# Attention with the values stationary, two heads in the column halves of TensorE, and the division ahead of the transpose

## The chip, the cores and the metric

The kernel runs on one core of one Trainium2 chip. The metric is the device time of one execution in microseconds (us). Engines: PE (matmuls, and PEld for its weight loads), DVE (vector), ACT (scalar), POOL and SP (here they only issue DMAs). Each works through its own queue in order; they meet at semaphores.

## The reference, cut to what matters

Two layers work on 256 latent and 256 context tokens. Attention is one of three branches of the token mixer:

```
s = einsum('bqhd,bkhd->bhqk', q, k) * SOFTMAX_SCALE   # 8 heads, 96 deep
p = softmax(s, axis=-1)
o = einsum('bhqk,bkhd->bqhd', p, v)                   # v is 64 wide per head
```

Latent queries see all 512 keys, context queries only the 256 context keys. In layer 0 both kinds of queries are computed, in layer 1 only the latent ones. After the attention come the gMLP branch, gates, projections, and a dense SwiGLU (layer 0) or a top-2-of-8 mixture of experts (layer 1), all of them many f32-by-parts matmuls.

## The kernel before

Activations lie transposed: channels on partitions, tokens in the free direction. The projections run as weight-stationary tiles; each product is three fp32r matmuls (L650 to L652, high and low parts). Weights come by DMA into `raw`, ACT rounds them (`whi`, L1187), DVE makes the remainder (`wlo`, L1567). DVE also has the taps of a depthwise convolution (L1652) to do, a fixed number (`TAPS_UNIT`, 1 in layer 0 and 3 in layer 1) in each step of the attention.

The attention of a layer is a list of units (`UNITS`), one for a pair of heads j, a head h of the pair and a tile t of 128 queries, in the order j, h, t: 32 units in layer 0 (four tiles: two with 512 keys, two with 256), 16 in layer 1 (all 512 keys). A unit passes these stages:

- scores (PE, `scores`, L851): queries stationary, keys moving, into one of two banks `sc_bank`
- row maximum and its negative (DVE, L1771, L1772)
- exponential with the row sum (ACT, L1353) into `pr`, which has two buffers; it waits until the unit two before has been turned (`pt_psum`)
- reciprocal of the row sum (DVE, L1780) into `rinv`
- turn (PE, `turn`, L860): transposes of 128 columns each into the one bank `TB`; it waits for the exponential and for the copy of the last turned unit (`pt_ready`)
- copy of the turned block to `pT` (ACT, L1346), two buffers
- values (PE, `values`, L873): `pT` stationary, V (64 columns of one head) moving, out as queries x 64
- scaling by `rinv` on the way to `otok` (ACT, L1365)
- once for each pair of heads: the pair's outputs turned (PE, `outputs`, L882) into an accumulator bank, and split to `oh` (ACT, L1369) and `ol` (DVE, L1786) for the output projection

The stages are staggered by hand. In step s PE does scores(s), turn(s-2), outputs of a pair if it is complete, values(s-3), the query projection of the next pair (`queries`, in three steps of a layer), and in the first 24 steps of layer 0 and all 16 unit steps of layer 1 a piece of the modulation (`mod_chunk`, L750), whose rows are turned every eighth step (L759). ACT does in step s: the copy of turned unit s-2, the exponential of unit s, the scaling of unit s-3, the output's high part, then the query copies. DVE: maximum of s, reciprocal of s-1, taps, the output's low part, query rotation. Semaphore counts run on from layer 0 to layer 1 (`base_u`).

A form that matters later stands in the spatial step (L952): `vtok`, 64 columns wide, is stationary and its products go to the lower or the upper 64 partitions of a bank.

Of the kernel before, what the change touches and what calls it, by code (L numbers as in the profile page):

```python
# [135 lines left out]
def plan():  # L136
# [3 lines left out]
    for L in range(LAYERS):  # L140
# [8 lines left out]
        for j in range(4):  # L149
            chunks.append(("uq", L, j))  # L150
            accs += [("uq", L, j, h) for h in range(2)]
            if j == 0:
                chunks.append(("uv", L))
                accs += [("uv", L, t) for t in range(4)]

            if j > L:
                accs.append(("ot", L, j - 1 - L))
        accs += [("ot", L, j) for j in range(3 - L, 4)]
# [55 lines left out]
def build(nc, A, out):  # L214
    with ExitStack() as ctx:
# [81 lines left out]

        otok = place("otok", [P, 4, P], F32, std_at)
# [139 lines left out]
        ot_psum = sem("ot_psum")  # L438
# [65 lines left out]
        UNITS = {L: [(j, h, t) for j in range(4) for h in range(2) for t in range(live(L) // P)]  # L504
# [11 lines left out]

        def output_pair(L, s):

            j, r = divmod(s - 3, pair_units(L))
            return j - 1 if r == 0 and 1 <= j <= 4 else None  # L520
# [124 lines left out]
        def _(pe):  # L645
# [119 lines left out]
            for L in range(LAYERS):  # L765
# [75 lines left out]
                def scores(u):  # L841
                    j, h, t = units[u]
                    if (h, t) == (0, 0):
# [10 lines left out]
                def turn(u):  # L854
                    lo, hi = keys_of(units[u][2])
                    pe.wait_ge(exp_ready, base_u + u + 1)
# [6 lines left out]
                def values(u):  # L863
                    j, h, t = units[u]
                    lo, hi = keys_of(t)
                    nk = (hi - lo) // P
                    if u == 0:
                        taken(pe, ("uv", L, 3))
                    pe.wait_ge(pt_ready, base_u + u + 1)
                    if base_u + u >= 2:  # L870
                        pe.wait_ge(o_ready, base_u + u - 1)
                    for i in range(nk):
                        mm = pe.matmul(o_bank[u % 2][:, 0:VH], pT[:, u % 2, i * P:(i + 1) * P],  # L873
                                       V[:, lo // P + i, (2 * j + h) * VH:(2 * j + h + 1) * VH],
                                       start=(i == 0), stop=(i == nk - 1))
                    mm.then_inc(o_psum, 1)

                def outputs(j):
                    pe.wait_ge(o_ready, base_u + (j + 1) * pair_units(L))
                    b = bank(("ot", L, j))  # L880
                    for t in range(nq // P):
                        mm = pe.transpose(b[:, t * P:(t + 1) * P], otok[:, t, :], ident[:])  # L882
                    mm.then_inc(ot_psum, 1)
# [14 lines left out]
                for s in range(len(units) + 4):  # L898
                    if s < len(units):
                        scores(s)  # L900
                    if 2 <= s <= len(units) + 1:
                        turn(s - 2)
                    if output_pair(L, s) is not None:
                        outputs(output_pair(L, s))
                    if 3 <= s <= len(units) + 2:
                        values(s - 3)
# [268 lines left out]
        def _(act):  # L1175
# [74 lines left out]
            for L in range(LAYERS):  # L1250
# [86 lines left out]
                for s in range(len(units) + 4):  # L1337
                    if s and s % KD == 0 and s // KD <= len(MOD_ATT[L]):
                        copy_rows(MOD_ATT[L][s // KD - 1])
                    if 2 <= s <= len(units) + 1:  # L1340
                        u = s - 2
                        lo, hi = keys_of(units[u][2])
                        act.wait_ge(pt_psum, base_u + u + 1)
                        if base_u + u >= 2:
                            act.wait_ge(o_psum, base_u + u - 1)
                        nc.scalar.copy(pT[:, u % 2, 0:hi - lo], TB[:, 0:hi - lo]).then_inc(pt_ready, 1)  # L1346
# [9 lines left out]
                    out_j = output_pair(L, s)  # L1356
                    if out_j is not None:

                        act.wait_ge(ot_psum, 4 * L + out_j + 1)
                    if 3 <= s <= len(units) + 2:  # L1360
                        u = s - 3
                        j, h, t = units[u]
# [804 lines left out]
```

## Time and profile before

| | |
|---|---|
| median of 3 runs | 2468.6 us (2468.12 to 2473.57) |
| the profiled execution | 2469.17 us, span 2467.2 us |
| PE busy | 2354.1 us (95%) |
| DVE busy | 1715.1 us (70%) |
| ACT busy | 1358.4 us (55%) |
| attention of layer 0 | from 145.36 us to 236.76 us of the span |
| attention of layer 1 | from 1054.17 us to 1118.25 us of the span |

Busy time is the union of an engine's instructions. A matmul's end is modelled and matmuls overlap in the pipeline, so what a group of matmuls costs is read from the start of one group to the start of the next, not from its duration. Clock 1.00 is 2.4 GHz, 0.50 is 1.2 GHz.

### The profile page before, as it was taken

How to read it: one execution, taken by the hardware profiler on the slowest of the kernel's cores; microseconds unless marked ns; L12 is line 12 of the kernel's file. 1: busy time of each engine (PE TensorE's matmuls, PEld its weight loads, DVE VectorE, ACT ScalarE, POOL GpSimd, SP SyncE). 2: the span in 40 equal slices, each digit the busy share in tenths (PEclk: the TensorE clock that was granted, in tenths of full speed). 3: DMA queues.
4: the chain of work that ended last, by engine and by line, in shares of the span. 5: the costliest groups of instructions: out<-in, count | busy, mean ns of one | idle time of the engine just before them, and what ended most of it. 6: DMA issues, size and time to landing. Idle time of an engine off the chain costs nothing.

```text
span 2467.2 us, 32689 instructions
## 1 busy us (share of the span) xinstructions
PE 2354.1 (95%) x12370; PEld 1921.1 (78%) x12370; DVE 1715.1 (70%) x1796; ACT 1358.4 (55%) x1438; POOL 46.1 (2%) x87
## 2 busy tenths in 40 slices
PE   6989999998999998898997999999999999999997
PEld 3757778876788885767995888888888888888886
DVE  4867753426333336777657989898989898989895
ACT  3366343234222234546446777777777777777773
POOL 0010000001000000010000000000000000000000
PEclk9999999999999999999997999999999999999999
DMA  7243123345422233433655999999999999999992
GB/s 281 86 138 125 59 98 102 116 163 207 141 96 94 95 102 121 153 129 124 197 215 199 368 350 365 346 361 358 364 346 367 346 369 352 361 351 362 346 369 105
DMA packets 103249, 569.02 MB, mean 231 GB/s; under 512 B 11760, under 2 KB 13680, under 8 KB 54640
## 3 DMA queue, kind: packets, MB, share of 16 engines
q1 hardware_dynamic: 91632, 525.72, 57.4%
q0 software_dynamic: 11520, 41.95, 4.7%
q8 instruction: 67, 1.10, 0.2%
q14 instruction: 30, 0.25, 0.0%
HBM read 566.58 MB, written 1.05 MB: 230 GB/s over the span
## 4 chain that ended last, share of the span: by engine, by line
PE 88%; DVE 6%; ACT 3%; issue 1%; SPq 1%; DMA 1%; DVEq 0%; ACTq 0%
PE bank L650 26%; PE bank L651 26%; PE bank L652 26%; PE bank L851 1%; PE bank L1070 1%; PE bank L873 1%; PE bank L1136 1%; PE bank L750 1%; DVE hres L1627 1%; PE bank L860 1%; DMA mod_s<-in_mod 1%; DVE y L1624 1%; DVE cacc L1652 1%; DVE wlo L1567 1%; SPq L545 0%
## 5 line engine op out<-in xcount | busy, mean ns | idle before, releaser
L1894 DVE TENSOR_TENSOR elo<-eraw,ehi 128x2048 fp32r<-128x2048 f32 x378 | 862.4, 2288 | 131.7 <-ACT ehi L1239 130.7
L1239 ACT CAST ehi<-eraw 128x2048 fp32r<-128x2048 f32 x378 | 722.6, 1915 | 246.1 <-PE bank L652 241.8
L1567 DVE TENSOR_TENSOR wlo<-raw,whi 128x1024 fp32r<-128x1024 f32 x220 | 269.5, 1225 | 244.4 <-ACT whi L1187 242.6
L650 PE MATMUL bank<-ah,whi 128*128 128x512 f32 (+1 forms) x1088 | 395.4, 363 | 12.2 <-DVE wlo L1567 6.5
L650 PE MATMUL bank<-ehi,xgh 128*128 128x512 f32 x1008 | 399.4, 396 | 1.7 <-DVE xgl L1900 1.2
L651 PE MATMUL bank<-elo,xgh 128*128 128x512 f32 x1008 | 393.4, 390 | 0.0
L652 PE MATMUL bank<-ehi,xgl 128*128 128x512 f32 x1008 | 393.0, 390 | 0.0
L651 PE MATMUL bank<-al,whi 128*128 128x512 f32 (+1 forms) x1088 | 389.9, 358 | 0.0
L652 PE MATMUL bank<-ah,wlo 128*128 128x512 f32 (+1 forms) x1088 | 389.8, 358 | 0.0
L1187 ACT CAST whi<-raw 128x1024 fp32r<-128x1024 f32 x220 | 229.3, 1043 | 117.5 <-PE bank L652 117.1
L650 PEld LDWEIGHTS bank<-ah,whi 128*128 128x128 f32 x1088 | 207.7, 191 | 47.4 <-DVE wlo L1567 10.2
L651 PEld LDWEIGHTS bank<-al,whi 128*128 128x128 f32 x1088 | 207.9, 191 | 30.5 <-issue 1.4
L652 PEld LDWEIGHTS bank<-ah,wlo 128*128 128x128 f32 x1088 | 207.8, 191 | 29.9
L652 PEld LDWEIGHTS bank<-ehi,xgl 128*128 128x128 f32 x1008 | 189.5, 188 | 41.0
L650 PEld LDWEIGHTS bank<-ehi,xgh 128*128 128x128 f32 x1008 | 189.6, 188 | 40.5 <-DVE xgl L1900 1.4
L651 PEld LDWEIGHTS bank<-elo,xgh 128*128 128x128 f32 x1008 | 189.6, 188 | 37.5
L650 PE MATMUL bank<-ehi,hTh 128*128 128x512 f32 x504 | 197.1, 391 | 1.5 <-DVE hTl L2019 1.5
L652 PE MATMUL bank<-ehi,hTl 128*128 128x512 f32 x504 | 196.2, 389 | 0.0
L651 PE MATMUL bank<-elo,hTh 128*128 128x512 f32 x504 | 196.0, 389 | 0.0
L1652 DVE SCALAR_TENSOR_TENSOR cacc<-up,par,cacc 128x512 f32<-128x512 f32 (+1 forms) x240 | 140.7, 612 | 3.1
L650 PEld LDWEIGHTS bank<-ehi,hTh 128*128 128x128 f32 x504 | 94.6, 188 | 21.0 <-issue 1.7
L652 PEld LDWEIGHTS bank<-ehi,hTl 128*128 128x128 f32 x504 | 94.6, 188 | 19.8
(268 smaller groups left out, 2685.1 us busy)
## 6 DMA issues: line engine op xcount, KB each, us to landing
eraw<-in_moe SPq DMA_DIRECT2D x378, 1024.0 KB, 5.1
raw<-in_dense SPq DMA_DIRECT2D x220, 512.0 KB, 3.3
mod_a<-in_mod POOLq DMA_DIRECT2D x40, 512.0 KB, 4.2
mod_b<-in_mod POOLq DMA_DIRECT2D x40, 512.0 KB, 7.5
mod_s<-in_mod SPq DMA_DIRECT2D x16, 512.0 KB, 13.5
hres<-in_xT SPq DMA_DIRECT2D x1, 2048.0 KB, 8.0
wsT<-in_wsT SPq DMA_DIRECT2D x2, 512.0 KB, 3.5
out_h<-hres SPq DMA_DIRECT2D x2, 512.0 KB, 2.9
```

What stands on the lines that cost most here:

```text
L650: pe.matmul(dst, wh, xh, start=first, stop=False, skip_group_check=True)
L651: pe.matmul(dst, wh, xl, start=False, stop=False, skip_group_check=True)
L652: return pe.matmul(dst, wl, xh, start=False, stop=last, skip_group_check=True)
L750: mm = pe.matmul(b[32 * j:32 * j + 32, :], cst[:, k, :], w[:, 256 * j:256 * j + 256], start=(k == 0), stop=(k == KD - 1), skip_group_check ...
L851: pe.matmul(sc_bank[u % 2][:, 0:hi - lo], qT_of(j)[:, h, t * P:(t + 1) * P], kT[:, 2 * j + h, lo:hi], start=True, stop=True).then_inc(sc_r ...
L860: mm = pe.transpose(TB[:, i * P:(i + 1) * P], pr[:, u % 2, i * P:(i + 1) * P], ident[:])
L873: mm = pe.matmul(o_bank[u % 2][:, 0:VH], pT[:, u % 2, i * P:(i + 1) * P], V[:, lo // P + i, (2 * j + h) * VH:(2 * j + h + 1) * VH], start= ...
L1187: nc.scalar.copy(whi[c % SPLIT][:], raw[c % RAW][:]).then_inc(w_hi, 1)
L1239: nc.scalar.copy(ehi[c % ESPLIT][:], eraw[c % ERAW][:]).then_inc(e_hi, 1)
L1567: dve.tensor_tensor(wlo[c % SPLIT][:], raw[c % RAW][:], whi[c % SPLIT][:].bitcast(F32), ALU.subtract).then_inc(w_lo, 1)
L1652: ins = dve.scalar_tensor_tensor(acc, src, w, acc, ALU.mult, ALU.add)
L1894: dve.tensor_tensor(elo[c % ESPLIT][:], eraw[c % ERAW][:], ehi[c % ESPLIT][:].bitcast(F32), ALU.subtract).then_inc(e_lo, 1)
```

## The change

- Units come in the order j, t, h: both heads of a pair for one tile of queries follow each other. In layer 0 four units with 512 keys are followed by four with 256.
- The exponentials are scaled by `rinv` in place (ACT, with its own semaphore `pn_ready`) before they are turned. The turn waits for that instead of the exponential.
- Values handles two units at once, in even steps from step 4: V is stationary (64 columns), `pT` moves (128 columns), head 0 goes to the lower 64 partitions of the output bank and head 1 to the upper ones. The output is then already channels x queries.
- `outputs`, `otok` and the accumulator banks for it are gone. ACT copies the bank to `oh` for each pair of units, DVE subtracts to `ol`.
- ACT's order in a step: exp(s), scale(s-1), copy of turned s-2, output copy (even steps). DVE's: reciprocal(s-1), maximum(s), output remainder (odd steps from 5), taps. PE's: scores(s), values (even steps), turn(s-2), queries, modulation.
- The loop has one step less.

```diff
-UNITS = {L: [(j, h, t) for j in range(4) for h in range(2) for t in range(live(L) // P)]
+UNITS = {L: [(j, h, t) for j in range(4) for t in range(live(L) // P) for h in range(2)]
          for L in range(LAYERS)}
...
         def turn(u):
             lo, hi = keys_of(units[u][2])
-            pe.wait_ge(exp_ready, base_u + u + 1)
+            pe.wait_ge(pn_ready, base_u + u + 1)
             if base_u + u:
                 pe.wait_ge(pt_ready, base_u + u)
             for i in range((hi - lo) // P):
                 mm = pe.transpose(TB[:, i * P:(i + 1) * P], pr[:, u % 2, i * P:(i + 1) * P], ident[:])
             mm.then_inc(pt_psum, 1)
 
-        def values(u):
-            j, h, t = units[u]
+        def values(m):
+
+            j, _, t = units[2 * m]
             lo, hi = keys_of(t)
             nk = (hi - lo) // P
-            if u == 0:
+            if m == 0:
                 taken(pe, ("uv", L, 3))
-            pe.wait_ge(pt_ready, base_u + u + 1)
-            if base_u + u >= 2:
-                pe.wait_ge(o_ready, base_u + u - 1)
+            pe.wait_ge(pt_ready, base_u + 2 * m + 2)
+            if base_u // 2 + m >= 2:
+                pe.wait_ge(o_ready, base_u // 2 + m - 1)
             for i in range(nk):
-                mm = pe.matmul(o_bank[u % 2][:, 0:VH], pT[:, u % 2, i * P:(i + 1) * P],
-                               V[:, lo // P + i, (2 * j + h) * VH:(2 * j + h + 1) * VH],
-                               start=(i == 0), stop=(i == nk - 1))
+                for h in range(2):
+                    mm = pe.matmul(o_bank[m % 2][64 * h:64 * h + 64, 0:P],
+                                   V[:, lo // P + i, (2 * j + h) * VH:(2 * j + h + 1) * VH],
+                                   pT[:, h, i * P:(i + 1) * P], start=(i == 0), stop=(i == nk - 1),
+                                   skip_group_check=True)
             mm.then_inc(o_psum, 1)
-
-        def outputs(j):
-            pe.wait_ge(o_ready, base_u + (j + 1) * pair_units(L))
-            b = bank(("ot", L, j))
-            for t in range(nq // P):
-                mm = pe.transpose(b[:, t * P:(t + 1) * P], otok[:, t, :], ident[:])
-            mm.then_inc(ot_psum, 1)
 
         base_u = 0 if L == 0 else len(UNITS[0])
...
-        for s in range(len(units) + 4):
+        for s in range(len(units) + 3):
             if s < len(units):
                 scores(s)
+            if s >= 4 and s % 2 == 0:
+                values(s // 2 - 2)
             if 2 <= s <= len(units) + 1:
                 turn(s - 2)
-            if output_pair(L, s) is not None:
-                outputs(output_pair(L, s))
-            if 3 <= s <= len(units) + 2:
-                values(s - 3)
             if s and query_pair(L, s) is not None:
                 queries(query_pair(L, s))
...
-        for s in range(len(units) + 4):
+        for s in range(len(units) + 3):
             if s and s % KD == 0 and s // KD <= len(MOD_ATT[L]):
                 copy_rows(MOD_ATT[L][s // KD - 1])
-            if 2 <= s <= len(units) + 1:
-                u = s - 2
-                lo, hi = keys_of(units[u][2])
-                act.wait_ge(pt_psum, base_u + u + 1)
-                if base_u + u >= 2:
-                    act.wait_ge(o_psum, base_u + u - 1)
-                nc.scalar.copy(pT[:, u % 2, 0:hi - lo], TB[:, 0:hi - lo]).then_inc(pt_ready, 1)
             if s < len(units):
 
                 lo, hi = keys_of(units[s][2])
...
                 nc.scalar.activation(pr[:, s % 2, 0:hi - lo], sc_bank[s % 2][:, 0:hi - lo], ACT.Exp,
                                      bias=negmax[:, s % 2:s % 2 + 1], scale=SCALE,
                                      accum_out=rsum[:, s % 2:s % 2 + 1]).then_inc(exp_ready, 1)
-            out_j = output_pair(L, s)
-            if out_j is not None:
-
-                act.wait_ge(ot_psum, 4 * L + out_j + 1)
-            if 3 <= s <= len(units) + 2:
-                u = s - 3
-                j, h, t = units[u]
+            if 1 <= s <= len(units):
+                u = s - 1
+                lo, hi = keys_of(units[u][2])
                 act.wait_ge(rinv_ready, base_u + u + 1)
-                act.wait_ge(o_psum, base_u + u + 1)
-                nc.scalar.activation(otok[:, t, 64 * h:64 * h + 64], o_bank[u % 2][:, 0:VH], ACT.Copy,
-                                     scale=rinv[:, u % 4:u % 4 + 1]).then_inc(o_ready, 1)
-            if out_j is not None:
-                b = acc_bank[ACC[("ot", L, out_j)] % 2]
-                nc.scalar.copy(oh[:, out_j, 0:nq], b[:, 0:nq]).then_inc(x_hi, 1)
+                nc.scalar.activation(pr[:, u % 2, 0:hi - lo], pr[:, u % 2, 0:hi - lo], ACT.Copy,
+                                     scale=rinv[:, u % 4:u % 4 + 1]).then_inc(pn_ready, 1)
+            if 2 <= s <= len(units) + 1:
+                u = s - 2
+                lo, hi = keys_of(units[u][2])
+                act.wait_ge(pt_psum, base_u + u + 1)
+                if base_u + u >= 2:
+                    act.wait_ge(o_psum, (base_u + u) // 2)
+                nc.scalar.copy(pT[:, u % 2, 0:hi - lo], TB[:, 0:hi - lo]).then_inc(pt_ready, 1)
+            if s >= 4 and s % 2 == 0:
+                m = s // 2 - 2
+                j, _, t = units[2 * m]
+                act.wait_ge(o_psum, base_u // 2 + m + 1)
+                nc.scalar.copy(oh[:, j, t * P:(t + 1) * P], o_bank[m % 2][:, 0:P]).then_inc(x_hi, 1)
             if s and query_pair(L, s) is not None:
                 take_queries(query_pair(L, s))
...
         taps(TAPS_IN["uv"][L])
         for s in range(len(units) + 4):
+            if 1 <= s <= len(units):
+                u = s - 1
+                dve.wait_ge(exp_ready, base_u + u + 1)
+                if base_u + u >= 4:
+
+                    dve.wait_ge(pn_ready, base_u + u - 3)
+                dve.reciprocal(rinv[:, u % 4:u % 4 + 1], rsum[:, u % 2:u % 2 + 1]).then_inc(rinv_ready, 1)
             if s < len(units):
                 lo, hi = keys_of(units[s][2])
                 i = s % 2
...
                 chain(dve.tensor_reduce(rowmax[:, i:i + 1], sc_bank[i][:, 0:hi - lo], AX.X, ALU.max))
                 dve.tensor_scalar(negmax[:, i:i + 1], rowmax[:, i:i + 1], -SCALE, None,
                                   ALU.mult).then_inc(negmax_ready, 1)
-            if 1 <= s <= len(units):
-                u = s - 1
-                dve.wait_ge(exp_ready, base_u + u + 1)
-                if base_u + u >= 4:
-
-                    dve.wait_ge(o_ready, base_u + u - 3)
-                dve.reciprocal(rinv[:, u % 4:u % 4 + 1], rsum[:, u % 2:u % 2 + 1]).then_inc(rinv_ready, 1)
+            if s >= 5 and s % 2 == 1:
+                m = (s - 5) // 2
+                j, _, t = units[2 * m]
+                dve.wait_ge(x_hi, n.next(x_hi))
+                dve.tensor_tensor(ol[:, j, t * P:(t + 1) * P], o_bank[m % 2][:, 0:P],
+                                  oh[:, j, t * P:(t + 1) * P].bitcast(F32), ALU.subtract).then_inc(o_ready, 1)
             taps(TAPS_UNIT[L])
-            out_j = output_pair(L, s)
-            if out_j is not None:
-                dve.wait_ge(x_hi, n.next(x_hi))
-                a = ACC[("ot", L, out_j)]
-                dve.tensor_tensor(ol[:, out_j, 0:nq], acc_bank[a % 2][:, 0:nq],
-                                  oh[:, out_j, 0:nq].bitcast(F32), ALU.subtract).then_inc(acc_free[a % 2], 1)
             if s and query_pair(L, s) is not None:
                 turn_queries(query_pair(L, s))
         modulation(L, *((16, 40), (32, 48))[L])
```

## Rows read from the trace of the kernel before

**Rows 1.** The chain of waits of the whole run, share of the span by engine.

```profile
PE 88%; DVE 6%; ACT 3%; issue 1%; SPq 1%; DMA 1%; DVEq 0%; ACTq 0%
```

**Rows 2.** Windows of both stages: length, busy PE, PEld, DVE, ACT, POOL; granted clock; DMA.

```profile
145.36:236.76 91.40, 88.43 (x629) 61.55 (x627) 64.70 (x160) 55.25 (x152) 11.13 (x21) 0.98 0.42 141
...
1054.17:1118.25 64.08, 58.90 (x424) 40.32 (x422) 54.99 (x137) 32.49 (x81) 6.89 (x13) 0.95 0.43 147
```

**Rows 3.** Timeline of PE, layer 0: start, duration (us), engine, line, operation, count.

```profile
178.23 0.60 PE L860 MATMUL bank<-ident,pr 128*128 128x128 f32 x4
178.66 0.60 PE L882 MATMUL bank<-ident,otok 128*128 128x128 f32 x4
...
181.79 1.00 PE L873 MATMUL bank<-V,pT 128*128 128x64 f32 x8
182.72 0.64 PE L750 MATMUL bank<-mod_a,cst 128*32 128x256 f32 x8
183.29 1.12 PE L851 MATMUL bank<-kT,qT 96*128 96x512 f32 x2
184.25 0.38 PE L860 MATMUL bank<-ident,pr 128*128 128x128 f32 x2
```

**Rows 4.** Timeline, spatial step of layer 0, PE alone.

```profile
302.87 1.09 PE L952 MATMUL bank<-wsT,vtok 128*64 128x128 f32 x16 [1.00 <-DVE uT L1825]
...
303.89 0.50 PE L650 MATMUL bank<-ah,whi 128*128 128x512 f32 x1
```

**Rows 5.** Groups of ACT by form, 145 to 312: busy us, mean ns, idle before.

```profile
L1353 ACT ACTIVATE pr<-bank,negmax 128x512 f32<-128x512 f32 x16 | 11.0, 688 | 8.2 <-DVE negmax L1772 8.2
...
L1346 ACT COPY pT<-bank 128x512 f32<-128x512 f32 x16 | 9.4, 586 | 6.5 <-PE bank L860 6.2
L1353 ACT ACTIVATE pr<-bank,negmax 128x256 f32<-128x256 f32 x16 | 7.7, 481 | 4.4 <-PE bank L860 2.9 <-DVE negmax L1772 1.4
...
L1346 ACT COPY pT<-bank 128x256 f32<-128x256 f32 x16 | 6.0, 372 | 11.5 <-PE bank L860 11.5
...
L1388 ACT ACTIVATE vT<-vT,par 128x512 f32<-128x512 f32 x4 | 2.9, 808 | 0.0
...
L1402 ACT CAST gmh<-uT 128x512 fp32r<-128x512 f32 x4 | 2.5, 621 | 8.0 <-DVE uT L1825 8.0
```

**Rows 6.** Timeline of ACT, layer 0: two instructions that follow each other.

```profile
223.21 0.31 ACT L1365 ACTIVATE otok<-bank,rinv 128x64 f32<-128x64 f32 x1
223.41 0.58 ACT L1346 COPY pT<-bank 128x512 f32<-128x512 f32 x1
```

**Rows 7.** Timeline, later in layer 0: transposes after a wait, and their reader.

```profile
292.05 0.66 PE L943 MATMUL bank<-ident,vT 128*128 128x128 f32 x4 [0.68 <-ACT vtok L1394]
292.75 0.59 ACT L1394 COPY vtok<-bank 128x512 f32<-128x512 f32 x1 [0.74 <-PE bank L943]
```

**Rows 8.** Timeline, layer 0: maximum and exponential of the scores at 183.29.

```profile
184.45 0.69 DVE L1771 TENSOR_REDUCE rowmax<-bank 128x1 f32<-128x512 f32 x1 [1.07 <-PE bank L851]
...
185.37 0.69 ACT L1353 ACTIVATE pr<-bank,negmax 128x512 f32<-128x512 f32 x1 [0.32 <-DVE negmax L1772]
```

**Rows 9.** Timeline of ACT: exp(0) of layer 0, exp(2) of layer 1.

```profile
150.22 0.69 ACT L1353 ACTIVATE pr<-bank,negmax 128x512 f32<-128x512 f32 x1 [2.48 <-DVE negmax L1772]
...
1067.74 0.69 ACT L1353 ACTIVATE pr<-bank,negmax 128x512 f32<-128x512 f32 x1 [3.44 <-DVE negmax L1772]
```

**Rows 10.** Timeline: first query matmul and next exponential, layer 0, then layer 1.

```profile
160.97 0.48 PE L650 MATMUL bank<-cnh,whi 128*128 128x512 f32 x1
...
169.04 0.47 ACT L1353 ACTIVATE pr<-bank,negmax 128x256 f32<-128x256 f32 x1 [1.45 <-DVE negmax L1772]
...
1076.97 0.36 PE L650 MATMUL bank<-cnh,whi 128*128 128x256 f32 x1
...
1083.71 0.69 ACT L1353 ACTIVATE pr<-bank,negmax 128x512 f32<-128x512 f32 x1 [1.66 <-DVE negmax L1772]
```

**Rows 11.** Windows, a stretch early in layer 1's attention; columns as in Rows 2.

```profile
1068.00:1077.00 9.00, 8.34 (x37) 5.73 (x37) 6.57 (x20) 4.30 (x12) 0.53 (x1) 0.62 0.35 119
```

More of the change, by code:

```diff
@@ L154, in plan @@
                 accs += [("uv", L, t) for t in range(4)]
-            if j > L:
-                accs.append(("ot", L, j - 1 - L))
-        accs += [("ot", L, j) for j in range(3 - L, 4)]
         for s in ("gv", "gu"):
@@ L296, in build @@
         qT2 = place("qT2", [QK_HEAD, 2, TOK], F32, wsT_at)
-        otok = place("otok", [P, 4, P], F32, std_at)
         uT = place("uT", [P, 4, TOK], F32, w1)
@@ L437, in build @@
         o_ready = sem("o_ready")
-        ot_psum = sem("ot_psum")
+        pn_ready = sem("pn_ready")
         vt_ready = sem("vt_ready")
@@ L515, in query_pair @@
             return j if r == 0 and 1 <= j < 4 else None
-        def output_pair(L, s):
-            j, r = divmod(s - 3, pair_units(L))
-            return j - 1 if r == 0 and 1 <= j <= 4 else None
         def qT_of(j):
@@ L842, in scores @@
                     j, h, t = units[u]
-                    if (h, t) == (0, 0):
+                    if (t, h) == (0, 0):
                         taken(pe, ("uk", L, 3))
```

## The prediction

> **What bounds the kernel now.** I read the chain of waits first: 88% of it is PE [rows 1]. The busy times of the two stretches that the change touches, the attention of layer 0 and of layer 1, come next: PE is busy for 88.4 of 91.4 us and 58.9 of 64.1 us, ACT for 55.2 and 32.5 [rows 2]. So PE sets the pace of attention in layer 0, and nearly so in layer 1. In the timeline of PE one step is scores, turn, values and a piece of modulation, back to back: eight value matmuls (512 keys) hold PE 0.93 us, a modulation piece 0.57 [rows 3]. I call what PE does for 512 keys L and for 256 keys S; layer 0 has 16 of each, layer 1 has 16 L.
>
> **The part that gets cheaper.** Values of two heads become 16 matmuls on 64-column halves. The form exists already in the spatial step: 16 such instructions start at 302.87 and the next full-width matmul starts at 303.89, so 1.02 us for a pair L where 2 x 0.93 were spent [rows 3, 4]. For a pair S I take 0.59, eight instructions less at (1.09 - 0.27)/15 = 0.054 us (0.27 is an estimate of the last one's own tail). PE work saved: layer 0 8 x 0.84 + 8 x 0.35 = 9.5 us, layer 1 8 x 0.84 = 6.7. The turns of the outputs go: four transposes are 0.43 us when nothing is waited for [rows 3], about 1.8 us in layer 0; in layer 1, where PE stops for the last scaling ahead of them, I estimate 3 us with that stop. Together 21 us of PE's time. The question is whether PE still is what is waited for.
>
> The row of the 64-column form has its change of layout in it: the next weight load starts only when the 16 have left the array, while between full-width matmuls a load is drawn ahead. The Trainium skill (TensorEngine Tiling (Array Packing), Key Properties) says that changing the tiling mode drains the array; the trace agrees. Without such a drain a pair L would cost 16 x 0.054 = 0.86 and the sum below would be 24 x 0.16 = 3.8 us less.
>
> **The part that gets slower: one chain through ACT.** In the new order ACT does in step s: exp(s), scale(s-1), the copy of the turned block pT(s-2), and in even steps the copy of an output. Three waits close this to a ring. exp(s) overwrites the buffer of unit s-2, so it waits for turn(s-2). turn(s-2) waits for the copy pT(s-3), since there is one bank for turned blocks, and for scale(s-2). Both stand behind exp(s-1) in ACT's queue. Before, the copy stood ahead of the exponential, so that ring was only turn and copy. Now no two steps overlap: turn(u-1) -> exp(u+1) -> scale(u) -> pT(u-1) -> turn(u). In even steps the values of a pair stand on PE between the copy and the turn, and need that copy, so they are in the ring too. What stands behind ACT's wait: everything of the next step, and through exp, DVE's reciprocal, behind which the next row maximum now stands.
>
> The terms, L / S. Exponential 0.69 / 0.48, copy of the turned block 0.59 / 0.37 [rows 5]. Scale, SBUF to SBUF in place with one scale column: the trace has no such row. The plain cast from SBUF is 0.62, the activation from SBUF with both a scale and a bias column is 0.81, so one column is half of the way, 0.72 [rows 5]; an ACT instruction that nobody waits for lets the next one start 0.11 us before its end (otok 0.31 long, next one 0.20 later) [rows 6], so 0.61 of ACT's queue; for S I estimate 0.39. Bounds: 0.20 (the 64-column scale, same operation) and 0.81. A turn that starts after a wait, to the start of ACT's work on it: 292.05 to 292.75, 0.70 [rows 7]; S two transposes less, 0.48. From ACT to PE 0.05.
>
> - L after L, odd unit: 0.70 + 0.69 + 0.61 + 0.59 + 0.05 = 2.64; even unit, with values: 3.66. A pair L takes 6.30 us.
> - S after S: 0.48 + 0.48 + 0.39 + 0.37 + 0.05 = 1.77, with values 2.36.
> - The mixed ones of a group of eight (four L, four S): 2.43, 3.23, 1.98, 2.79. One group: 20.9 us.
>
> PE's own work for a pair L is 2 x 0.96 scores, 2 x 0.43 turns, 1.02 values, 2 x 0.57 modulation = 4.9 us, so it is idle for a fifth even where it has modulation to do. The way over the row maximum, 1.16 us from the start of the scores to the reduction and 0.92 from there to the exponential [rows 3, 8], is at 0.59 + 0.57 + 2.08 = 3.2 us after the turn's start, against 0.70 + 2.64 = 3.3 on the ring: hidden, but only just. Where an L follows an S it is late by 0.5, with a modulation's row turn ahead of it by 1.0; I add 3 us in layer 0 and 0.4 in layer 1. DVE's reciprocal ahead of the reduction costs nothing: exponential to exponential through DVE is 0.8 + 0.05 + 0.08 + 0.92 = 1.85.
>
> **Layer 0.** exp(0) stays at 150.22 [rows 9]; the reciprocal and maximum behind it put exp(1) at 152.0, its scale(0) ends at 153.4, and the first turn starts at 153.5, 8.1 us into the stage. Four groups 83.4, less the last interval (2.8) and the exponential missing at the end (0.7): 79.9. Queries three times: they start 0.43 after a turn, and from their first matmul to the next exponential it is 8.07 (160.97 to 169.04), since ACT and DVE must turn the queries first [rows 10]; to the next turn 1.29 more. Together 9.8 us in place of 3.23 + 1.77, so 4.8 each, 14.4. Row maximum 3. End: copy, values S, 1.5 us, and no turn of outputs. Sum 8.1 + 79.9 + 14.4 + 3.0 + 1.5 = 106.9 against 91.4 [rows 2]: +15.5 us.
>
> **Layer 1.** exp(2) is at 1067.74 [rows 9], 0.6 later with scale(0) ahead of the query copies; turn(1) follows at 1070.25, 16.1 us into the stage. PE waits for it, and its granted clock is low afterwards, as it already is there today (0.62 over 1068 to 1077 [rows 11]); a turn and values at half rate on the ring add 1.9. Seven pairs 44.1 less 0.7. Two queries inside: 0.43 + 6.74 (1076.97 to 1083.71) [rows 10] + 1.94 = 9.1 in place of 6.3, 5.6 together. Row maximum 0.4, end 2.4. Sum 16.1 + 1.9 + 43.4 + 5.6 + 0.4 + 2.4 = 69.8 against 64.1: +5.7.
>
> **Moved but free.** DVE's subtractions become 24 of 128 columns where there were 8 larger ones; they stand in steps where DVE waits for the scores. ACT's output copy runs beside the next turn. The accumulator banks lose four users in a layer, which keeps their alternation for all later work. SP and POOL lose nothing: POOL's modulation fetches follow PE's pieces with 3 buffers. After attention PE is the bound again, and its weights, ACT's rounding and DVE's remainders all hang on it, so a later end moves everything by its full amount.
>
> Total +21.2 us on the profiled execution (2469.2 us, span 2467.2): 2490. The median of the runs shown, 2468.6, is 0.6 lower, so I say 2490.
>
> **Rivals.**
> 1. PE stays the bound, the ring hides. Then the 21 us of PE work come off: 2469 - 21 = 2448. For it: PE is 97% busy in layer 0 now, ACT 60%. Against: ACT's order leaves it nothing to do while it waits for the turn. It would need a step L of at most 2.4 us on average where the ring has 3.15. Chance 0.06.
> 2. The scale costs no more than the 64-column one. 48 x 0.41 = 20 us come off: 2470, no change. For it: the same operation; against: all of ACT's rows grow with their columns, 0.37 to 0.59 for the copy. Chance 0.06.
> 3. PE's clock falls as well. The ring leaves PE 20 to 40% idle. The granted clock is 0.98 and 0.95 of 2.4 GHz over the stages today [rows 2], and 0.62 where PE had waited for exp(2) of layer 1, which itself waited 3.4 us for its maximum [rows 9, 11]. At 1.2 GHz throughout, turns and values on the ring would add 20 us in layer 0 and 14 in layer 1: 2524; in parts of the stages, 2500. Chance of more than 10 us of it: 0.16.
> 4. The forecast, 2480 to 2498: 0.72. Its own range is made by the scale's cost (48 x 0.15 = 7 us either way), the drain (4) and shorter drops of the clock.
>
> **The numbers.** Likeliest 2490. The range reaches down by the cheaper scale and halves to 2476 and up into the third rival to 2503. A measurement of this kernel can tell 0.2% (5 us) from no change. Faster than that: rival 1, 0.06, and a bit of 2, 0.01. The same: 0.05 from rival 2. Slower: 0.88.
>
> **What would show it.** In the timeline after, exp(s) starts right after turn(s-2) in every step, and the copy pT is the last thing before each turn; waits of ACT for the turn, over 20 us in layer 0; PE waiting for pT and for the scaled block, which it hardly does today. A pair L 6.3 us from turn to turn, values 1.0 us for a pair, the scale 0.7 us. Stages of 107 and 70 us. It is wrong if PE is still over 90% busy in the stages, if a scale is under 0.4 us, or if the later stages take back part of the delay.

## The result and the profile after

The changed kernel takes 2507.2 us (median of four, 2500.4 to 2518.5) against 2470.5 for the kernel before (median of four, 2468.1 to 2473.6): ratio 1.0152, 95% interval 1.0136 to 1.0168. It is slower, as forecast, but by 37 us where 21 had been forecast, and lies beyond the range's upper end of 2503. The profiled execution took 2507.76 us, with a span of 2505.9.

| | before | after | forecast |
|---|---|---|---|
| stage of layer 0 | 91.4 | 120.0 | 106.9 |
| stage of layer 1 | 64.1 | 77.1 | 69.8 |
| the rest of the span | 2311.7 | 2308.8 | as before |

A stage runs from the first scores to the first matmul of the next part. The delay is all in these two stages. First their windows, with a stretch of each kind (columns as in [rows 2]), then the chain of waits (as [rows 1]):

```profile
144.44:264.42 119.98, 97.47 (x611) 51.29 (x609) 68.37 (x171) 63.51 (x164) 11.08 (x21) 0.85 0.33 109
1082.10:1159.20 77.10, 62.08 (x416) 33.66 (x414) 55.61 (x139) 38.29 (x85) 6.86 (x13) 0.85 0.37 127
172.00:184.00 12.00, 11.16 (x48) 4.71 (x48) 5.28 (x15) 5.40 (x18) 1.58 (x3) 0.57 0.43 132
204.00:216.00 12.00, 11.82 (x56) 4.82 (x55) 5.17 (x13) 4.74 (x14) 1.58 (x3) 0.58 0.38 120
157.00:172.00 15.00, 12.36 (x100) 7.71 (x92) 8.80 (x23) 8.47 (x21) 2.11 (x4) 1.00 0.36 123
```

```profile
PE 86%; DVE 6%; ACT 5%; issue 2%; SPq 1%; DMA 1%; DVEq 0%; ACTq 0%
```

PE was busy for 97% of layer 0's stage and is now for 81%. The granted clock, 0.98 and 0.95 in [rows 2], is 0.85 in both stages. It isn't low everywhere: over 157 to 172 it is 1.00, over 172 to 184 and 204 to 216, both behind a block of queries, 0.57 and 0.58, so most of those stretches ran at 1.2 GHz. That is the first sign of what the forecast left out.

The ring is there as forecast. The groups of ACT by form, layer 0, which answer to [rows 5]:

```profile
L1336 ACT ACTIVATE pr<-pr,rinv 128x512 f32<-128x512 f32 x16 | 11.3, 709 | 0.0
L1329 ACT ACTIVATE pr<-bank,negmax 128x512 f32<-128x512 f32 x16 | 11.0, 687 | 26.8 <-PE bank L849 15.0 <-DVE negmax L1759 11.8
L1344 ACT COPY pT<-bank 128x512 f32<-128x512 f32 x16 | 9.1, 572 | 0.0
L1336 ACT ACTIVATE pr<-pr,rinv 128x256 f32<-128x256 f32 x16 | 8.0, 497 | 0.0
L1329 ACT ACTIVATE pr<-bank,negmax 128x256 f32<-128x256 f32 x16 | 7.6, 473 | 24.9 <-PE bank L849 16.2 <-DVE negmax L1759 8.7
```

The scale is 709 ns where I had taken 0.72 us. ACT, idle 8.2 and 4.4 us before its exponentials in [rows 5], is now idle 26.8 and 24.9. Most of it, 31 us, waits for the turn, as the ring has it, but 20.5 wait for the row maximum. Two steps of the ring at full clock, PE and ACT in layer 0:

```profile
184.26 0.66 PE L864 MATMUL bank<-pT,V 128*64 128x128 f32 x8
184.85 0.66 PE L849 MATMUL bank<-ident,pr 128*128 128x128 f32 x4
...
185.60 0.69 ACT L1329 ACTIVATE pr<-bank,negmax 128x512 f32<-128x512 f32 x1 [1.39 <-PE bank L849]
...
186.28 0.71 ACT L1336 ACTIVATE pr<-pr,rinv 128x512 f32<-128x512 f32 x1
...
186.89 0.57 ACT L1344 COPY pT<-bank 128x512 f32<-128x512 f32 x1
...
187.61 0.63 PE L849 MATMUL bank<-ident,pr 128*128 128x128 f32 x4 [0.48 <-ACT pT L1344]
...
188.33 0.69 ACT L1329 ACTIVATE pr<-bank,negmax 128x512 f32<-128x512 f32 x1 [0.70 <-PE bank L849]
...
190.25 1.09 PE L864 MATMUL bank<-pT,V 128*64 128x128 f32 x16 [0.81 <-ACT pT L1344]
191.27 0.44 PE L849 MATMUL bank<-ident,pr 128*128 128x128 f32 x2
```

Turn, exponential, scale, copy, turn: 187.61 - 184.85 = 2.76 us where 2.64 was forecast. With the values, 191.27 - 187.61 = 3.66, as forecast. The same kind of steps after a block of queries:

```profile
175.21 1.06 PE L840 MATMUL bank<-kT,qT 96*128 96x512 f32 x1
176.20 1.12 PE L864 MATMUL bank<-pT,V 128*64 128x128 f32 x8
177.25 0.69 PE L849 MATMUL bank<-ident,pr 128*128 128x128 f32 x2
177.73 0.86 PE L748 MATMUL bank<-sel,modrow 128*128 128x8 f32 x4
178.52 1.08 PE L739 MATMUL bank<-mod_a,cst 128*32 128x256 f32 x8
179.54 2.08 PE L840 MATMUL bank<-kT,qT 96*128 96x512 f32 x2
181.41 0.64 PE L849 MATMUL bank<-ident,pr 128*128 128x128 f32 x2
```

Every PE row is about twice as long: scores 2.0 us, a piece of the modulation 1.0. This S step takes 181.41 - 177.25 = 4.16 us where the forecast has 1.98, and 1.0 for the modulation's row turn in it. PE has no gap in it: turn 0.48, row turn 0.79, piece 1.02, scores 1.87. With the clock held up (the shorter extra matmuls below) the same two turns are at 174.23 and 176.69, 2.46 apart, with one extra matmul of 0.22 between them.

### The profile page after: what moved, and what is told of

It is laid out like the page before. It is cut to its first block, busy times and chain, and to the rows that moved or that the text cites. A ratio compares the mean times of both kernels' runs of the same rounds, so it can differ in the third digit from the quotient of the medians.

```text
span 2505.9 us, 32587 instructions
## 1 busy us (share of the span) xinstructions
PE 2364.8 (94%) x12346; PEld 1901.5 (76%) x12346; DVE 1719.8 (69%) x1812; ACT 1371.3 (55%) x1454; POOL 45.9 (2%) x87
## 4 chain that ended last, share of the span: by engine, by line
PE 86%; DVE 6%; ACT 5%; issue 2%; SPq 1%; DMA 1%; DVEq 0%; ACTq 0%
PE bank L639 26%; PE bank L641 25%; PE bank L640 25%; PE bank L1053 1%; PE bank L1119 1%; PE bank L849 1%; PE bank L864 1%; PE bank L840 1%; DVE hres L1607 1%; ACT pr L1336 1%; PE bank L739 1%; DVE wlo L1547 1%; ACT pT L1344 1%; DMA mod_s<-in_mod 1%; DVE y L1604 1%
## 5 line engine op out<-in xcount | busy, mean ns | idle before, releaser
L639 PEld LDWEIGHTS bank<-ah,whi 128*128 128x128 f32 x1088 | 207.9, 191 | 49.0 <-DVE wlo L1547 10.2
L639 PE MATMUL bank<-ehi,hTh 128*128 128x512 f32 x504 | 197.1, 391 | 1.5 <-DVE hTl L1999 1.5
```

The costliest lines, as they stand in the source:

```text
L639: pe.matmul(dst, wh, xh, start=first, stop=False, skip_group_check=True)
```

## The experiments

Each version below the first row was timed in five rounds beside the kernel before, whose median lay at 2470.4 to 2471.2. Stages, in us, are from the windows of each version's one profiled execution.

| | kernel, us | ratio (95%) | stage 0 | stage 1 |
|---|---|---|---|---|
| as changed | 2507.2 | 1.0152 (1.0136 to 1.0168) | 120.0 | 77.1 |
| extra matmuls on PE, long | 2498.3 | 1.0114 (1.0100 to 1.0129) | 114.5 | 70.6 |
| extra matmuls, shorter | 2495.2 | 1.0087 (1.0070 to 1.0105) | 109.3 | 69.7 |
| third buffer | 2502.5 | 1.0133 (1.0118 to 1.0148) | 114.3 | 75.8 |
| scores one step earlier | 2509.9 | 1.0152 (1.0137 to 1.0167) | 118.8 | 79.1 |
| both | 2476.8 | 1.0023 (1.0014 to 1.0032) | 94.3 | 67.1 |
| third buffer, chunk first | 2488.1 | 1.0065 (1.0051 to 1.0079) | 108.4 | 77.5 |
| scale of one column | 2490.9 | 1.0085 (1.0072 to 1.0098) | 110.0 | 70.2 |
| copy, scale, exp | 2464.2 | 0.9977 (0.9969 to 0.9986) | 88.8 | 61.2 |
| the same, scores earlier | 2539.6 | 1.0270 (1.0245 to 1.0294) | 135.2 | 87.3 |
| the same, extra matmuls | 2459.5 | 0.9950 (0.9936 to 0.9963) | 88.4 | 58.2 |
| division on DVE | 2472.6 | 1.0009 (1.0000 to 1.0018) | 88.8 | 68.0 |
| before, extra matmuls | 2463.2 | 0.9964 (0.9950 to 0.9977) | 89.6 | 60.8 |

### Is it the clock?

```
+ def warm(s, k):
+     for _ in range(k):
+         pe.matmul(b[:, 384:512], ident[:], ident[:], ...)
  scores(s)
+ warm(s, spare(s))        # s >= 2; and 12 (4) ahead of scores(2)
  values(s // 2 - 2); turn(s - 2)
```

> The changed kernel with extra fp32 matmuls of 128 columns (0.147 us each at the full clock, written to a part of a bank nobody reads) put on PE where it stands idle in the attention stages: 12 before scores(2), 5 after it, 8 before the turn that follows a query block, 4 or 2 in the steps with modulation, 7 in those without, in layer 1 up to 18; 80% of the measured idle time at most. Theory A (the ring through ACT costs what was forecast, and the 17 us beyond the forecast are steps run at PE's 1.2 GHz level, into which PE falls because it idles): the windows of the attention stages show a granted clock near 1.00, layer 0's stage takes about 107 us instead of 120.0, layer 1's 72 instead of 77, and the kernel 2490 us. Rival B (the low clock is no cause: the ring has a cost not counted, such as the row maximum behind the scores): the stage stays at 118 us or more and the kernel at 2507 or above, slower by what the extra matmuls get in the way.

Measured: the clock is 1.00 in both stages, and the kernel is at 2498.3, between the two theories. Layer 1's stage is 70.6 (Theory A: 72), layer 0's 114.5 instead of 107. In the window of layer 0 PE was busy for 112.7 of 114.5 us, which left no room: an extra matmul takes 0.245 us, and 0.147, the price of a transpose, had been used. (In this version they also start a new sum in the bank that holds the modulation's running sums, and this version computes another result; the versions below only add to theirs. The Trainium skill, PSUM — Partial Sum Buffer, The four PSUM rules, says that a starting matmul clears the marks of the whole bank, whichever bytes it writes; no run here shows that by itself, since the next version also has fewer of them.) So it was repeated with fewer:

```
- spare(s): 8 behind a query block, 4 or 2 with a chunk, 7 without; 12 ahead of scores(2)
+ spare(s): 5, 2 or 1, 3; 8 ahead of scores(2)
- start=True, stop=True
+ start=False, stop=False
```

> The changed kernel with extra matmuls on PE again, now by their measured length (0.245 us for each, where 0.147 had been counted, so that the earlier version had PE busy for 128 of 130 us and stood in its own way): 2 ahead of the values, 1 ahead of the other turns, 5 in the step behind a query block, 3 in the steps without modulation, 8 ahead of scores(2) in layer 0. Theory A (half of the excess over the forecast is PE at its lower level): layer 0's stage 107 to 110 us (120.0 as changed, 114.5 with the longer filling), layer 1's 70 to 71, the kernel 2488 to 2493. Rival B (the longer filling took all that the clock had to give): 2498 again or more.

```profile
144.31:253.62 109.31, 98.61 (x761) 65.51 (x759) 67.83 (x171) 63.53 (x164) 11.08 (x21) 1.00 0.36 120
1069.57:1139.28 69.71, 61.96 (x505) 39.90 (x503) 55.73 (x139) 38.30 (x85) 6.86 (x13) 1.00 0.41 139
```

These are the two stages: 109.3 and 69.7 us at clock 1.00, as Theory A has them. More work on PE makes the stages 18.1 us shorter, 197.1 to 179.0. That leaves 2.4 us of layer 0's excess over the forecast and, since the forecast of 69.8 has 1.9 us of half clock in it, 1.8 us in layer 1. The whole kernel came out at 2495.2, 12.0 us below the changed kernel and 2 us above what Theory A gave. The 18.1 us are those of the profiled execution, one of the two shortest; the five runs spread from 2488.0 (the profiled one, mean clock 0.986) to 2496.2 (0.983), and where the longer ones lost 7 us no trace shows.

### Which link closes the ring?

```
- exp(s) into pr[s % 2], waits for turn(s-2)
+ exp(s) into one of three buffers, waits for turn(s-3)
```

> The changed kernel with a third buffer for the exponential (in the space that the outputs' tile had before the change), so that exp(s) waits for turn(s-3) and not for turn(s-2); ACT's order stays. Theory A (the ring is closed by exp's wait for the buffer, and ACT's order inside it): the link is cut, exp(s) starts right after the last copy, ACT's own work of 0.69 + 0.71 + 0.57 + 0.14 = 2.1 us a step is below PE's 2.7, and the kernel is at 2450 to 2465 as with the other order. Rival B (ACT's added work): 2498 or above. Rival C (the buffer is not what exp waits for, but the copy's place behind exp and scale): between the two, 2480 to 2495.

Theory A fell here. Rival B's number came, 2502.5, but not for its reason, ACT's added work. The group rows of ACT (its exponential, in two of the buffers) say why:

```profile
L1333 ACT ACTIVATE pr<-bank,negmax 128x512 f32<-128x512 f32 (+1 forms) x22 | 12.8, 583 | 30.1 <-DVE negmax L1763 30.1
...
L1333 ACT ACTIVATE prc<-bank,negmax 128x512 f32<-128x512 f32 (+1 forms) x10 | 5.8, 582 | 13.6 <-DVE negmax L1763 13.6
```

No wait for the turn is left, and all 43.7 us are for the row maximum, which waits for the scores, which stand on PE behind the last turn. There are two rings of nearly one length. The forecast had worked out both, 3.2 and 3.3 us from a turn to the next step's exponential, and called the second "hidden, but only just"; I should have seen that cutting the longer one buys only the difference. The other link alone, and then both:

```
- for s: scores(s);   values(..); turn(s-2); chunk
+ scores(0); for s: scores(s+1); values(..); turn(s-2); chunk
```

> The changed kernel with PE's scores one step earlier: scores(s+1) ahead of values and turn(s-2), where scores(s+1) stood behind turn(s-2) and the modulation's chunk. Theory A2 (two rings of the same length: one through exp's wait for its buffer, 6.3 us for two L steps; one through PE's order, copy, values 1.02, turn 0.59, chunk 0.57, scores 1.06, row maximum 0.9, exp 0.67, scale 0.62, copy 0.57, together 6.1 to 6.2): this cuts the second alone, the first still holds, 2495 to 2505, exp waits for the turn at nearly every step and no longer for the row maximum. Rival B (only the ring through the row maximum is real, the other is its shadow): PE bound again, 2455 to 2470.

> The changed kernel with both: scores one step earlier and the third buffer for the exponential. Theory A2: both rings are cut, and ACT's order of the change (exp, scale, copy) costs nothing by itself; PE is the bound where there is modulation, the stage of layer 0 is 88 to 93 us and the kernel 2458 to 2470, as with ACT's other order (2464). Rival B (there is a third link, such as the reciprocal ahead of the row maximum on DVE, or ACT's own work): 2480 or more, and the idle rows before exp name it.

```profile
L1330 ACT ACTIVATE pr<-bank,negmax 128x512 f32<-128x512 f32 (+1 forms) x32 | 18.6, 581 | 49.9 <-PE bank L849 37.7 <-DVE negmax L1760 12.2
```

```profile
144.60:238.91 94.31, 83.17 (x611) 46.46 (x610) 66.40 (x171) 64.05 (x164) 11.10 (x21) 0.96 0.44 141
1060.18:1127.23 67.05, 55.67 (x416) 31.39 (x414) 54.91 (x139) 39.02 (x85) 6.87 (x13) 0.90 0.42 146
```

The first row is the exponential with the scores earlier alone: 37.7 us of waiting for the turn, the first ring. The kernel is at 2509.9, a little worse than forecast, since scores(3) now stands on PE ahead of the first turn, which moves from 7.9 to 10.3 us into layer 0's stage. The windows are those of both edits: 2476.8, with stages of 94.3 us, where 88 to 93 had been expected, and 67.1. One cut alone gives back 5 us or none, both give 30. The kernel does 0.2% worse than before, above Theory A2's number and under Rival B's; the later first turn, here too 10.3 us into the stage, is part of it.

The third buffer once more, with the second ring shortened instead of cut:

```
- for s: scores(s); values(..); turn(s-2); queries; chunk
+ for s: scores(s); chunk; values(..); turn(s-2); queries
```

> The changed kernel with the third buffer (2502 by itself) and the modulation's chunk ahead of values and turn in PE's order, where it stood behind them. Theory A2 (with the third buffer the ring that holds is copy, values, turn, chunk, scores, row maximum, exp, scale, copy, 6.2 us for two L steps): the chunk, 0.57 a step, leaves that ring and fills PE's wait, 24 steps in layer 0 and 16 in layer 1; one chunk is in the ring per two steps, so 0.57 for each of 20 pairs, 11 us, and some 5 more because PE idles less and keeps its clock: 2483 to 2492. Rival B (the chunk had been hidden): 2500 again.

2488.1, as Theory A2 has it: with the third buffer, what PE does between copy and scores is part of the length of the second ring. The profiled execution is the slowest of six (2502.8, the others 2486.5 to 2490.3), so its windows in the table don't stand for the median.

### What the scale costs

```
- activation(pr[:, u % 2, 0:n], pr[:, u % 2, 0:n], Copy, scale=rinv)
+ activation(pr[:, u % 2, 0:1], pr[:, u % 2, 0:1], Copy, scale=rinv)
```

> The changed kernel with the scaling cut to one column of 512 or 256 (leaves the division of the other columns out; every wait and signal stays). Theory A: the ring loses 0.6 us in an L unit and 0.4 in an S unit, some 26 us over both layers, L odd 2.0 and even 3.05, pair L 5.1 under PE's 5.5: PE bound again where there is modulation, the clock stays up, and the kernel is at 2455 to 2475. Rival B (the turn's wait for the exponential's buffer and the copies alone hold the stage): 2490 or above.

This version leaves the division of all other columns out. 2490.9: 16 us come back, less than the 26 of Theory A, and Rival B's number, if only just. The clock is 0.86 and 0.85 in the two stages, unmoved, where the expectation had it stay up. The stages are 10.0 and 6.9 us shorter. ACT's one-column form still takes 283 ns, so of 0.71 and 0.50 us only 0.43 and 0.21 go: 16 x 0.426 + 16 x 0.214 = 10.2 for layer 0 and 6.8 for layer 1, which is what the stages show.

### ACT's order

```
- exp(s); scale(s-1); copy pT(s-2); copy oh
+ copy pT(s-2); scale(s-1); copy oh; exp(s)
```

> The changed kernel with ACT's order in a step turned round: copy pT(s-2), scale(s-1), copy to oh, exp(s), where it was exp(s), scale(s-1), pT(s-2), oh. Nothing else. Theory A (the time is set by the ring turn, exp, scale, copy, turn: 0.7 + 0.69 + 0.71 + 0.57 in an L step): exp and scale leave the ring, which is then turn and copy, 1.3 us, and PE is the bound again: an L step with modulation 1.06 + 0.59 + 0.57 + 0.51 = 2.7, an S step 1.8; the stage of layer 0 near 92 us, the kernel 2450 to 2465, with the clock back at 0.98 and PE waiting for pT in few steps. Rival B (what costs is ACT's own added work, 16 scales of 0.71 and 15 of 0.50 in the window of 120 us, with any order): under 10 us come back, 2498 or above. Rival C (the division ahead of the turn puts the reciprocal on the path: ACT now waits for DVE ahead of each scale, 0.3 to 0.5 us in 48 units): 2475 to 2485, and the wait before scale reads DVE.

2464.2, inside Theory A's numbers. All that the change does is still there, the scale's 0.7 us and ACT's added work too. What is different is that the exponential stands last: behind the copy, as before the change, and behind the scale and the output's copy too. That is worth 43 us; how much of it the copy's place brings by itself, without the scale's, no run shows. Both stages:

```profile
144.57:233.33 88.76, 82.24 (x611) 45.29 (x609) 65.50 (x171) 64.67 (x164) 11.07 (x21) 0.99 0.45 147
1051.03:1112.27 61.24, 53.81 (x416) 30.23 (x414) 54.87 (x140) 39.31 (x85) 6.86 (x13) 0.94 0.46 153
```

ACT is busy for 64.7 us, more than in the changed kernel (63.5), in a stage 31 us shorter. It is now 0.23% faster than before the change.

Both orders changed, ACT's as above and PE's with scores(s+1) ahead of values and turn(s-2), as in the diff of the scores above:

> ACT's order copy, scale, copy to oh, exp, and scores one step earlier on PE. Theory A2: with ACT's other order the row maximum has a step of room already (2.5 us of idle before exp in all of layer 0), so little is left to gain: 2460 to 2465. Rival C: the earlier scores take the wait for exp(s-1) ahead of the turn, which ACT's order now makes late, and PE loses 0.2 to 0.5 us a step: 2470 to 2485.

Rival C had the sign, and both sizes are far off: 2539.6. ACT and PE in layer 0:

```profile
187.90 0.70 ACT L1348 ACTIVATE pr<-bank,negmax 128x512 f32<-128x512 f32 x1
...
188.74 0.70 PE L840 MATMUL bank<-kT,qT 96*128 96x256 f32 x2 [1.56 <-ACT pr L1348]
...
189.28 0.60 PE L849 MATMUL bank<-ident,pr 128*128 128x128 f32 x4
...
189.91 0.59 ACT L1330 COPY pT<-bank 128x512 f32<-128x512 f32 x1 [1.23 <-PE bank L849]
190.40 0.72 ACT L1335 ACTIVATE pr<-pr,rinv 128x512 f32<-128x512 f32 x1
...
191.02 0.68 ACT L1348 ACTIVATE pr<-bank,negmax 128x512 f32<-128x512 f32 x1
```

ACT's order alone gave 43 us and the earlier scores nothing, and together they close a new ring: exp(s-1) is now the last thing in ACT's step, PE waits for it in front of scores(s+1), the turn stands behind these scores, and copy, scale and the next exponential behind the turn. 191.02 - 187.90 = 3.12 us a step, and more with values in it. The row maximum isn't in this ring: PE and ACT wait for each other in turn.

Next, ACT's order with extra matmuls in the places that are still idle:

```
+ s == 2: warm(s, (8, 3)[L]) ahead of scores(s)
+ behind scores(s): L == 0: 1 for s = 27 to 31, 2 from 32; L == 1: 12 for s = 3, 2 for s = 17, 18
```

> ACT's order copy, scale, copy to oh, exp (2464 by itself), with extra matmuls of 0.245 us only where PE still idles: 8 ahead of scores(2) in layer 0 (2.25 us idle there), 3 in layer 1 (0.88), 12 ahead of the second turn of layer 1 (3.87 idle), 1 or 2 in layer 0's last ten steps. Theory A (PE's lower level is a cost of its own wherever PE idles): the stretches at half clock behind these places (6 us of layer 1's stage behind the idle 3.87, 7 us behind the end of layer 0's stage) run at the full clock, worth about half of their length, 3 to 6 us together: 2458 to 2461. Rival B (they are hidden by something else): 2464 as without.

2459.5, as Theory A has it, the fastest version, 0.5% under the kernel before. Layer 1's stage went from 61.2 to 58.2, where the window behind the idle 3.87 us reads 0.66 without the extra matmuls and 1.00 with them. Layer 0's stage gains only 0.3, though over 224 to 240, around its end, the clock goes from 0.79 to 1.00.

And the kernel before the change with them:

```
+ ahead of scores(s): L == 0: 8 for s = 2; L == 1: 3, 2, 8 for s = 2, 3, 4
```

> The kernel before the change with extra matmuls where its PE idles at the start of the stages: 8 ahead of scores(2) in layer 0 (2.25 us idle), 3 ahead of scores(2) and 8 ahead of scores(4) in layer 1 (2.19 idle, with 9 us at half clock behind it). Theory A: layer 1's stage 61 to 62 us where it was 64.1, layer 0's 90 to 91, the kernel 2466 to 2469 where it was 2471. Rival B (no gain): 2471. It says how much of a gain of the filled version over the kernel before is the filling's.

2463.2, better than Theory A's number; layer 1's 60.8 and layer 0's 89.6 a little better than its ranges. So of the 11 us that the fastest version is under the kernel before, 7 are to be had without the change, and the change in its best order brings 3.7.

Last, the division off ACT:

```
- ACT: activation(pr, pr, Copy, scale=rinv) -> pn_ready
+ DVE, behind row maximum and reciprocal: tensor_scalar(pr, pr, rinv, mult) -> pn_ready
```

> The changed kernel with the division on DVE: the row maximum first, then the reciprocal, then the exponential times it, in DVE's queue; ACT's order is copy, copy to oh, exp, as without a scale. Theory A2 (no ring is closed through ACT, and DVE has the room: its multiply takes under 0.6 us, and it is 73% busy with the other order of ACT): PE bound in the steps with modulation, layer 0's stage 86 to 90 us, and in the steps without it ACT's 0.6 a step are gone: 2458 to 2465. Rival D (the multiply delays the row maximum and the convolution's taps on DVE, which then are late for the stage behind): 2468 to 2485, with DVE as the releaser before exp or behind the stage.

```profile
L1757 DVE TENSOR_SCALAR pr<-pr,rinv 128x512 f32<-128x512 f32 x16 | 7.8, 487 | 0.6
L1757 DVE TENSOR_SCALAR pr<-pr,rinv 128x256 f32<-128x256 f32 x16 | 5.7, 353 | 0.6
```

2472.6, inside Rival D's numbers. DVE takes 487 and 353 ns for what ACT takes 709 and 497. Layer 0's stage is 88.8 as with ACT scaling, and layer 1's is 68.0 against 61.2: DVE is busy for 61.7 of these 68.0 us, and PE waits 9.7 us there for the scaled block. It is layer 1 that makes Rival D right. The Trainium skill (Trainium Architecture — The Big Picture, The five engines, in one table) has DVE up to about three times as fast as ACT per element at simple arithmetic; here it was 709/487 = 1.5 for a block of 512.

## Why the prediction was right and wrong

**The bound and the ring: right, at full clock.** PE was the bound and isn't, and ACT's order sets the step. The exponential behind copy and scale gives all of it back.

**The terms of the ring: right.** 2.76 for 2.64, 3.66 for 3.66; values of a pair 1.02 for 1.02, of an S pair 0.59 (184.26 to 184.85) for 0.59; scale 0.71 and 0.50, of ACT's queue 0.61 (186.28 to 186.89) for 0.61; turn(3) to turn(5) over queries 10.0 (162.84 to 172.84) for 9.8; layer 0's first turn 7.9 us into its stage for 8.1; layer 1's turn(1) 16.3 (1082.10 to 1098.40) for 16.1. Run at full clock, the stages are 109.3 and 69.7; the forecast has 106.9 and, without its 1.9 us of half clock, 67.9. So these terms are short by 4.2 us together.

**The clock: the step that failed.** It stands in the forecast as "a turn and values at half rate on the ring add 1.9" in layer 1 and nothing in layer 0, and as rival 3, which had it in words but with a chance of 0.16 and 10 to 34 us. Measured by removing it, it is 18.1 us, 10.7 in layer 0 and 7.4 in layer 1, in the profiled executions (12.0 us between the medians of the whole kernel). With 15.5 + 5.7 = 21.2 forecast, 41.6 us were lost in the stages. The kernel before pays for its clock too: the extra matmuls take its stages from 155.5 to 150.4. With both kernels at full clock 28.6 us are lost, and 13.0 are what the change costs through the clock. The forecast had the evidence in hand: PE idle a fifth of its time on the ring, and a case [rows 11] in which PE had idled and ran at 0.62 for 9 us after. It should have been a term of the sum, and the likeliest case should have been rival 3's "in parts, 2500". The Trainium skill (TensorE: Matmul & The Clock Gate, A second HAM failure mode: psum-queue depth-cycling) reports it of another kernel: short idle pieces between groups of matmuls made the clock go back and forth between its two levels, and throughput paid for it. The trace here agrees on the going back and forth, with 1.00 over 157 to 172, 0.57 over 172 to 184 and 1.00 again over 184 to 196. I had not weighed it.

**What the low clock does: more than the forecast's term.** The forecast and its rival 3 let only a turn and values, what PE has on the ring, take twice as long. The rows show all of PE's work doubled, and then PE is the bound again: in the S step above turn, row turn, piece and scores fill 4.16 us without a gap, though scale and copy are long done, and over 204 to 216 PE is busy for 11.82 of 12 us. The 20 and 14 us that rival 3 gives for half clock throughout are too low for the same reason: PE's 82.2 us of work in layer 0's stage (with ACT's other order, at 0.99), doubled, would be 164 us, an estimate, where rival 3 has 106.9 + 20 = 127. The row maximum, hidden but for 3 us in the forecast, ends 20.5 us of ACT's idle time in layer 0's stage, and still 15.3 with the clock held up; what it costs by itself no run separates.

**PE's savings: too high.** I had counted 9.5 + 6.7 + 1.8 us; only rival 1's 2448 rests on them, not the 2490. With ACT's other order, where PE is nearly the bound, its busy time in the stages fell from 88.4 + 58.9 to 82.2 + 53.8, by 11.3. A pair L of layer 1 in that version, PE's timeline:

```profile
1095.76 1.12 PE L840 MATMUL bank<-kT,qT 96*128 96x512 f32 x2
1096.82 1.09 PE L864 MATMUL bank<-pT,V 128*64 128x128 f32 x16
1097.84 0.66 PE L849 MATMUL bank<-ident,pr 128*128 128x128 f32 x4
1098.43 0.64 PE L739 MATMUL bank<-mod_a,cst 128*32 128x256 f32 x8
1098.99 1.12 PE L840 MATMUL bank<-kT,qT 96*128 96x512 f32 x2
1099.96 0.60 PE L849 MATMUL bank<-ident,pr 128*128 128x128 f32 x4
1100.49 0.64 PE L739 MATMUL bank<-mod_a,cst 128*32 128x256 f32 x8
...
1102.12 1.09 PE L864 MATMUL bank<-pT,V 128*64 128x128 f32 x16
```

It is 5.30 us, not 4.9. The values are the 1.02 of the forecast, but scores that stand before them hold PE 1.06 instead of 0.96, and a turn that stands before a modulation's piece 0.59 or 0.53 instead of 0.43 before full-width values. So a change of tile shape was paid at each border, 0.10 to 0.16 us, and with the values moved the turn now borders on the 32-column form. The Trainium skill (TensorEngine Tiling (Array Packing), Key Properties) says that a change of tiling mode drains the array; the trace agrees, as far as the dearer borders go.

**The rest: right.** Outside the stages the span is 3 us shorter than before, less than the runs of one kernel differ, so no later part visibly took the delay back or added to it.

## What to carry to other kernels

When three engines pass a unit in a ring, write out each engine's order in a step and follow every ring of waits, the second longest too: here one more buffer or an earlier issue alone gave 5 us or nothing, both gave 30, and putting the exponential last in ACT's step gave 43 with no buffer at all. When a forecast has PE idle for a part of every step, put the clock's price into the sum, not among the rivals, and count all of PE's work of a step at it, not only the part on the ring. And test a clock theory by giving PE useless work in its idle places: less than fills them, since the longer filling left layer 0's stage 5 us longer than the shorter one. It was worth 7 us even in the kernel before.

## What the runs showed of the hardware

- An fp32 matmul with 128 moving columns takes 0.22 to 0.25 us of PE at full clock (in the longer filling four start at 207.36 and what follows at 208.34, eight start at 197.62 and what follows at 199.41); a transpose of a block as large takes 0.15 or less (0.59 for four).
- ACT's scaled copy from SBUF to SBUF: 709 ns for 512 columns, 497 for 256, 283 for one. The cut from 512 columns to one saves only 60% of it.
- In this trace PE's mean busy share in a stretch doesn't tell the clock: over 172 to 184 PE was busy for 93% of the time (with rows twice as long) at 0.57, over 157 to 172 for 82% at 1.00. Ahead of the low stretch PE had waited 1.47 us for the turn at 172.84.
